# RWKV scan of a hybrid diffusion step: level products over all 128 rows, and a new issue order

## The reference

```python
def step(S, inp):
    r_t, w_t, k_t, v_t, kk_t, a_t = inp
    sa = jnp.einsum('bdhvk,bdhk->bdhv', S, -kk_t)
    S = (S * w_t[..., None, :] + sa[..., None] * (kk_t * a_t)[..., None, :]
         + v_t[..., None] * k_t[..., None, :])
    return S, jnp.einsum('bdhvk,bdhk->bdhv', S, r_t)
```

## Time and profile before

| | us |
|---|---|
| median of 3 runs (lowest, highest) | 4503.6 (4500.49, 4511.37) |
| the profiled execution | 4488.36 |
| its span, first to last instruction | 4486.5 |
| TensorE multiplying | 4088.9 (91%) |
| TensorE loading weights | 3518.4 (78%) |
| VectorE | 2644.1 (59%) |
| ScalarE | 1940.2 (43%) |
| GpSimd | 92.4 (2%) |
| mean granted TensorE clock | 0.966 of full speed |

### The profile page before, as it was taken

The page is one execution under the profiler, slowest core; times in us unless marked ns, Lnnn a source line. Parts: engine busy times, 40 slices in busy tenths (PEclk is TensorE's granted clock), DMA queues, the critical chain, the costliest instruction groups (busy, mean ns, idle before and its releaser), DMA issues. The chain is left out here.

```text
span 4486.5 us, 132472 instructions
## 1 busy us (share of the span) xinstructions
PE 4088.9 (91%) x58742; PEld 3518.4 (78%) x58742; DVE 2644.1 (59%) x4529; ACT 1940.2 (43%) x3640; POOL 92.4 (2%) x82
## 2 busy tenths in 40 slices
PE   6999978999988899899998999998999979999978
PEld 2888867888876799666668899886988868888858
DVE  6433557888866642455556433367524578888855
ACT  5333325666654531455554000045333256666642
POOL 0000000000110000000000000000000000001100
PEclk9999989999999899899999999999999989999989
DMA  8444765334434231100000222112345853334441
GB/s 314 145 127 134 221 206 147 101 104 103 99 68 158 79 70 41 53 1 1 2 15 24 98 95 71 43 62 69 114 124 174 255 163 107 103 107 100 92 151 59
DMA packets 541001, 470.96 MB, mean 105 GB/s; under 512 B 30096, under 2 KB 501264, under 8 KB 532752
## 3 DMA queue, kind: packets, MB, share of 16 engines
q1 hardware_dynamic: 389008, 386.96, 27.0%
q10 hardware_dynamic: 131840, 66.07, 5.1%
q0 software_dynamic: 19584, 9.44, 2.2%
HBM read 328.43 MB, written 128.71 MB: 102 GB/s over the span
## 5 line engine op out<-in xcount | busy, mean ns | idle before, releaser
L652 PE MATMUL ps<-big_r,stage_r 128*128 128x384 f32 x2976 | 638.8, 349 | 15.0 <-DVE big_r L914 13.6
L652 PEld LDWEIGHTS ps<-big_r,stage_r 128*128 128x128 f32 x2976 | 521.6, 189 | 69.2 <-issue 24.9
L2552 PE MATMUL ps<-big_r,w_out 128*128 128x384 f32 x2304 | 417.6, 341 | 36.1 <-DVE w_out L2668 35.8
L2552 PEld LDWEIGHTS ps<-big_r,w_out 128*128 128x128 f32 x2304 | 407.5, 191 | 44.6 <-DVE w_out L2668 38.8
L652 PE MATMUL ps<-big_r,w_slab_r 128*128 128x384 f32 x1488 | 340.6, 336 | 0.0
L369 PE MATMUL ps<-big_r,stage_r 128*128 128x384 f32 x1536 | 311.7, 337 | 13.2 <-DVE big_r L356 13.2
L2274 DVE TENSOR_REDUCE extra<-ps 128x1 f32<-128x1152 f32 (+1 forms) x144 | 177.7, 1234 | 204.0 <-PE ps L2179 204.0
L369 PEld LDWEIGHTS ps<-big_r,stage_r 128*128 128x128 f32 x1536 | 270.7, 189 | 27.8 <-issue 26.7
L1691 DVE COPY_PREDICATED arena<-arena,ps 128x128 f32<-128x128 uint32 x720 | 195.1, 328 | 123.6 <-PE ps L1305 121.1
L652 PEld LDWEIGHTS ps<-big_r,w_slab_r 128*128 128x128 f32 x1488 | 267.5, 189 | 0.0
L1513 ACT COPY arena<-ps 128x512 f32<-128x512 f32 x288 | 168.9, 586 | 205.1 <-PE ps L1319 204.9
(11 more groups left out here) (260 smaller groups left out, 8035.6 us busy)
## 6 DMA issues: line engine op xcount, KB each, us to landing
w_slab<-in_w SPq DMA_DIRECT2D x138, 512.0 KB, 3.3
arena<-scan_in SPq DMA_DIRECT2D x144, 320.0 KB, 3.7
arena<-scan_in SPq DMA_DIRECT2D x288, 128.0 KB, 3.7
scan_in<-x_resid ACTq DMA_DIRECT2D x48, 576.0 KB, 4.3
arena<-scan_in SPq DMA_DIRECT2D x48, 576.0 KB, 7.5
arena<-scan_in SPq DMA_DIRECT2D x144, 192.0 KB, 4.0
arena<-in_w_ada SPq DMA_DIRECT2D x24, 1024.0 KB, 5.9
x_resid<-in_w_ada SPq DMA_DIRECT2D x24, 1024.0 KB, 4.8
```

The costliest lines, as they stand in the source:

```text
L652: mm = pe.matmul(g.ps[:, 3 * s + c, 0:CW], w[:, k * P:(k + 1) * P], x[:, k, chunk(c)], start=k == i == 0, stop=k == NB - 1 and i == 2)
L2552: mm = pe.matmul(g.ps[:, bank(i, b), 0:wide[i]], w[:, b, k * P:(k + 1) * P], r, start=k == j == 0, stop=k == NB - 1 and j == 2)
```

## The change

The tile `xb` holds the inverse as a matrix with the two time halves on the diagonal and zeros beside them (cleared once by GpSimd), and `ba` holds the gram rows of both halves, one above the other, copied from `gr` by GpSimd (`copy_ba`, two copies of 64x512 for each pair). From level 2 on `level_u` is 8 products with 128 contracted rows, 64 output rows and 64 columns, and `level_x` (levels 2 to 4) likewise. `level_t` is 8 transposes of 64x128 in place of 4 of 128x128. `copy_x` becomes two copies, one for each half of the rows: 64x512 at level 1, 64x256 at levels 2 to 4. `level_w` at levels 2 to 4 is two masked copies of 64x256 instead of 128x128. Level 1's products, and `last_level_t`, stay. Both new tiles lie in the weight slab, which is idle in the scan.

```diff
+    xb = g.slab[:, 0, 0:1024]
+    ba = [g.slab[:, 1, 512 * i:512 * i + 512] for i in range(2)]
...
-            def level_u(q, k):
-                n = 1 << k
-                if k == 1:
-                    pe.wait_ge(x_ok, q + 1)
-                    if q:
-                        pe.wait_ge(w_ok, 10 * q)
-                if k == 5:
-                    pe.wait_ge(xa_ok, 4 * q + 4)
+            def first_u(q):
+                n = 2
+                pe.wait_ge(x_ok, q + 1)
+                if q:
+                    pe.wait_ge(w_ok, 10 * q)
+                    pe.wait_ge(xt_ok, 5 * q - 1)
...
                 for d, s in U8:
                     for h in range(2):
                         for p in range(2):
@@ -1307,28 +1308,50 @@
                                            strided(x, u * P + h * HD + d * n, (2 * n, 32 // n), (1, n), rows=HALVES[p]), start=True, stop=True)
                 mm.then_inc(u_mm, 1)
 
-            def level_x(q, k):
-                pe.wait_ge(w_ok, 10 * q + 2 * k)
-                if k == 1:
-                    pe.wait_ge(t1_ok, q + 1)
-                else:
-                    pe.wait_ge(xt_ok, 5 * q + k - 1)
+            def level_u(q, k):
+                n = 1 << k
+                if k == 2:
+                    pe.wait_ge(ba_ok, 2 * q + 2)
+                pe.wait_ge(xa_ok, 8 * q + 2 * k - 2)
+                for d, s in U8:
+                    for h in range(2):
+                        u = 2 * d + s
+                        mm = pe.matmul(strided(ps, u * HD, (1, HD), rows=HALVES[h]),
+                                       strided(ba[q % 2], (4 * h + u) * HD, (1, HD)),
+                                       strided(xb, u * P + h * HD + d * n, (512, 2), (2 * n, 32 // n), (1, n)), start=True, stop=True)
+                mm.then_inc(u_mm, 1)
+
+            def first_x(q):
+                pe.wait_ge(w_ok, 10 * q + 2)
+                pe.wait_ge(t1_ok, q + 1)
                 for d, s in U8:
                     for h in range(2):
                         for p in range(2):
                             mm = pe.matmul(strided(ps, h * 512 + (2 * d + s) * HD, (1, HD), rows=HALVES[p]),
                                            strided(xt[q % 2], lx(d, p, s), (1, HD), rows=HALVES[h]),
-                                           strided(wk(k), lx(d, p, s), (1, HD), rows=HALVES[h]), start=True, stop=True)
+                                           strided(wk(1), lx(d, p, s), (1, HD), rows=HALVES[h]), start=True, stop=True)
                 mm.then_inc(x_mm, 1)
 
+            def level_x(q, k):
+                pe.wait_ge(w_ok, 10 * q + 2 * k)
+                pe.wait_ge(xt_ok, 5 * q + k - 1)
+                for d, s in U8:
+                    for p in range(2):
+                        u = 2 * d + s
+                        mm = pe.matmul(strided(ps, 512 + u * HD, (1, HD), rows=HALVES[p]),
+                                       strided(xt[q % 2], lx(d, p, s), (1, HD)),
+                                       strided(wk(k), (2 * u + p) * HD, (1, HD)), start=True, stop=True)
+                mm.then_inc(x_mm, 1)
+
             def level_t(q, k):
 
-                if k < 4:
-                    pe.wait_ge(xa_ok, 4 * q + k)
                 if q and k == 1:
                     pe.wait_ge(xt_ok, 5 * q)
                 for d, s in U8:
-                    mm = pe.transpose(strided(ps, 2 * 512 + lx(d, 0, s), (P, 2), (1, HD)), strided(x, (2 * d + s) * P, (1, P)), g.ident[:, :])
+                    for p in range(2):
+                        u = 2 * d + s
+                        mm = pe.transpose(strided(ps, (1 + p) * 512 + u * HD, (1, HD)), strided(xb, p * 512 + u * P, (1, P), rows=HALVES[p]),
+                                          g.ident[HALVES[p], HALVES[p]])
                 mm.then_inc(t_mm, 1)
...
-            def tokens_v(q):
-                if q:
-                    pe.wait_ge(v_in[q % 4], 32 * loads(q, 4))
-                pe.wait_ge(t1_ok, q + 1)
-                for u in range(4):
-                    mm = pe.transpose(strided(ps, 3 * 512 + u * P, (1, P)), strided(vraw[q % 4], u * P, (1, P)), g.ident[:, :])
-                mm.then_inc(tok_mm, 1)
-
-            def tokens_bk(q):
-                if q >= 2:
+            def tokens(q, part):
+                if part == 0:
+                    if q:
+                        pe.wait_ge(v_in[q % 4], 32 * loads(q, 4))
+                    pe.wait_ge(t1_ok, q + 1)
+                if part == 2 and q >= 2:
                     pe.wait_ge(sum_ok, 2 * q - 2)
                 for u in range(4):
-                    mm = pe.transpose(strided(ps, 6 * 512 + u * P, (1, P)), strided(bk[q % 2], u * 256 + P, (1, P)), g.ident[:, :])
-                mm.then_inc(tok_mm, 1)
-                for u in range(4):
-                    mm = pe.transpose(strided(ps, 4 * 512 + u * P, (1, P)), strided(bk[q % 2], u * 256, (1, P)), g.ident[:, :])
+                    src = strided(vraw[q % 4], u * P, (1, P)) if part == 0 else strided(bk[q % 2], u * 256 + (part - 1) * P, (1, P))
+                    mm = pe.transpose(strided(ps, (3, 4, 6)[part] * 512 + u * P, (1, P)), src, g.ident[:, :])
                 mm.then_inc(tok_mm, 1)
...
             def copy_x(q, k):
+                n = 1 << k
                 act.wait_ge(x_mm, 4 * q + k)
-                A.copy(strided(x, 0, (HD, 2), (P, 4), (1, HD)), strided(ps, 0, (512, 2), (HD, 4), (1, HD))).then_inc(xa_ok, 1)
+                for p in range(2):
+                    rows = HALVES[p]
+                    if k == 1:
+                        if q == p == 0:
+                            act.wait_ge(blank_ok, 1)
+                        A.copy(strided(xb, p * 512, (HD, 2), (P, 4), (1, HD), rows=rows),
+                               strided(ps, 0, (512, 2), (HD, 4), (1, HD), rows=rows)).then_inc(xa_ok, 1)
+                    else:
+                        A.copy(strided(xb, p * 512, (256 + n, 2), (2 * n, P // n), (1, n), rows=rows),
+                               strided(ps, 512, (P, 2), (n, P // n), (1, n), rows=rows)).then_inc(xa_ok, 1)
 
...
-                    A.copy(strided(xt[q % 2], n, (256 - n, 2), (2 * n, P // n), (1, n)),
-                           strided(ps, 2 * 512 + n, (256 - n, 2), (2 * n, P // n), (1, n))).then_inc(xt_ok, 1)
+                    A.copy(strided(xt[q % 2], n, (P, 2), (256 - n, 2), (2 * n, HD // n), (1, n)),
+                           strided(ps, 512 + n, (512, 2), (P - n, 2), (2 * n, HD // n), (1, n))).then_inc(xt_ok, 1)
...
+            def chain_sa_half(c, step, d):
+                act.wait_ge(sa_mm, 2 * c + step + 1)
+                rows, t = HALVES[1 - tau(d, step)], tau(d, step)
+                A.copy(strided(sav[c % 2], t * 512 + d * 256, (HD, 2), (P, 2), (1, HD), rows=rows),
+                       strided(ps, 5 * 512 + d * P, (512, 2), (HD, 2), (1, HD), rows=rows)).then_inc(sav_ok, 1)
+
...
-                for p in range(2):
-                    V.copy_predicated(strided(wk(k), p * P, (256 + n, 2), (2 * n, HD // n), (1, n)),
-                                      bits(strided(level_mask, (k - 1) * P, (HD, 2), (n, HD // n), (1, n))),
-                                      strided(ps, p * 512, (HD, 2), (n, HD // n), (1, n))).then_inc(w_ok, 1)
+                for i in range(2):
+                    if k in (1, 5):
+                        src = strided(ps, i * 512, (HD, 2), (n, HD // n), (1, n)) if k == 1 else strided(ps, i * 32, (P, 2), (HD, 2), (1, 32))
+                        V.copy_predicated(strided(wk(k), i * P, (256 + n, 2), (2 * n, HD // n), (1, n)),
+                                          bits(strided(level_mask, (k - 1) * P, (HD, 2), (n, HD // n), (1, n))), src).then_inc(w_ok, 1)
+                    else:
+                        V.copy_predicated(strided(wk(k), i * 32, (256, 2), (HD, 4), (1, 32), rows=HALVES[i]),
+                                          bits(strided(level_mask, (k - 1) * P, (HD, 2), (0, 4), (1, 32), rows=HALVES[i])),
+                                          strided(ps, 0, (P, 2), (32, 4), (1, 32), rows=HALVES[i])).then_inc(w_ok, 1)
 
...
             nc.gpsimd.tensor_scalar(less, ch(g, "k_a", 8 * j, 8), -1.0, 1.0, ALU.mult, ALU.add).then_inc(less_ok, 1)
+
+            def copy_ba(q, t):
+                pool.wait_ge(g_ok, 4 * q + 2 * t + 2)
+                if q >= 2:
+                    pool.wait_ge(u_mm, 5 * q - 5)
+                rows = HALVES[1 - t]
+                nc.gpsimd.tensor_copy(strided(ba[q % 2], 0, (HD, 8), (1, HD), rows=rows),
+                                      strided(gr[q % 3], t * 1024, (P, 8), (1, HD), rows=rows)).then_inc(ba_ok, 1)
+
+            for q in range(2):
+                copy_ba(q, 0)
+                copy_ba(q, 1)
             for c in range(PAIRS):
+                if c + 2 < PAIRS:
+                    copy_ba(c + 2, 0)
+                    copy_ba(c + 2, 1)
                 if plain_stores(c) == 2:
                     continue
 
...
+            if k in (1, 5):
```

(24 more changed lines are left out.)

118 lines of the change are left out of this document (49 added, 69 removed).

## The result

The changed kernel takes 4390.6 us (median of 3 runs, 4390.2 to 4391.2), before 4503.6: a ratio of 0.9745 (95% interval 0.9726 to 0.9764), 2.5% less.

What follows compares the result with a forecast made beforehand. TensorE's list was taken to set the scan. Shortened to 16.4 us a pair, plus 1.0 new waits, 0.1 for VectorE and 0.95 hold-ups, it gave 18.45 for 18.82: -27 us over 72 pairs, 4476 us, range 4405 to 4550.

Steps and rivals of the forecast that it cites:

- my lower bound: TensorE's `level_t`: eight 64x128 transposes at 0.24 us if half the columns count half; 0.3 was taken, 0.47 the upper value.
- the sum: Three engine lists laid side by side: TensorE 16.4 us plus 1.0 of new waits, hold-ups added, 18.45 us a pair.
- The pair before: Scan period of the old kernel, 18.82 us: 17.3 without hold-ups in TensorE's groups, 1.5 lost to them.
- The clean pair, 17.5 forecast: Scan pair without hold-ups after the change: 17.5 us, 0.2 us longer than the old 17.3.
- 0.1 for a VectorE without slack: Added to the 17.4 us pair because VectorE would be busy for 16.8 of it: 0.1 us.
- 1.5 becomes 1.25 us: TensorE's hold-ups per pair shrink with its multiplies, 485 for 581: from 1.5 to 1.25 us.
- then 0.95: Hold-ups ahead of TensorE's new waits cost only what is over, taking a quarter off: 0.95 us a pair.
- (2): Hold-ups fall more than in proportion, or transposes take 0.24: 17.9 us a pair, 4437 us, down to 4410; chance 0.13.
- (4): VectorE's list takes over the scan: 19.1 to 19.4 us a pair, 4524 to 4546 us; chance 0.22.
- (5): GpSimd's copies disturb VectorE while they run: could be +0.7, so 19.2 us a pair, 4531 us; chance 0.08.
- (6): Undone row tiles on TensorE are missed, `u` groups double: +1.8 us a pair, +130 us, 4634 us; chance 0.03.
- takes 1.5 us out of a chain with slack: Putting `u` ahead of `t` in three levels cuts some 1.5 us from the level chain, grown from 12.5 to 14.9.

Runs made afterwards that it cites:

- e8: Kernel before, with two wide 256-column products into unused columns ahead of both the level 3 and level 4 products; 4581.9 us.
- e5: Kernel before, with two wide 256-column products into unused columns ahead of the level 4 product only; time grew by 43 us.
- e4: Changed kernel with each new level product split into two of 32 columns, same data and order; 4585.5 us.
- e7: Changed kernel with VectorE's 128x512 subtraction of the decays made by GpSimd; time the same as the changed kernel's, clean pair 16.83 us for 17.12.
- e6: Changed kernel with two wide 256-column products into unused columns ahead of the level 4 product; 4454.4 us.

## Why the prediction was wrong

- **Right: what bounds it, and the small terms.** TensorE's list set the pace. Multiplies a pair are 484 for 580, 96 fewer as counted. `level_w` takes 0.91 for 0.95, GpSimd's copy 0.61 for 0.7 and is hidden, TensorE waits for the two-part copies 11.1 us in 340 for some 15 in 380. The transposes take 0.24, my lower bound, where I took 0.3: 0.24 us a pair. TensorE's waits for data come to 1.0 us a pair (20.0 us in 340), as in the sum. The start of a scan costs nothing, as I had put it. The pair before was sized well, too: 17.3 and 1.5 us of hold-ups for 17.45 and 1.45.
- **The clean pair, 17.5 forecast, is 17.12.** The transposes are 0.24 of it; I had also added 0.1 for a VectorE without slack, which was not needed. The rest, 0.04, is open. That is 27 us.
- **The step that failed is "1.5 becomes 1.25 us", then 0.95.** I let the hold-ups fall with the count of instructions. Measured above the clean pair they are 0.34 us. The e8, e5 and e4 kernels show that the count is not what they follow: they fall when almost the same instructions are spread over a longer pair, and don't return with 596 multiplies at 60 records a us. Before, TensorE went through its list at 66 a us when nothing stopped it; the changed kernel asks for 57. Their 0.6 us below my value are 43 us. Together with the clean pair's 27 this makes the difference in the profiled executions, 4461 forecast for 4390.2.
- **The rival that came true is (2)**, with the lowest transposes and hold-ups that fall more than in proportion; I gave it 0.13 and priced it with 0.6 us of hold-ups at 4437, down to 4410; measured is 19 us less still, as both its clean pair (17.3) and its hold-ups were too large. Its "for" named the clock; a granted clock of 0.99 to 1.00 in both windows says that this is a small part.
- **(4) didn't come.** VectorE did get to 95%, but its waits for TensorE shrank with it, from 66 us to 21 between 900 and 1280 us; taking 0.6 us off it gained nothing in the time (e7). Neither list sets the pair alone: +1.06 us on TensorE's list costs 0.86 (e6), and -0.6 on VectorE's list gives 0.29 in the clean pair (e7).
- **(5) and (6) didn't come.** In the changed kernel hardly any of VectorE's products of two memory inputs runs beside GpSimd's copies, and the masked copies of a level that do take 0.437 us for 0.440 without. In e7 one such product runs beside GpSimd's subtraction and is no longer than before (0.683 us for 0.685), so the contention that the Trainium skill names (GPSIMD Engine Reference, Specifications) is not seen in it. Undoing the row tiles cost no time, since the groups over 64 rows had 16 products where the new ones have 8; at equal counts it does cost, as e4 shows, 57 ns a product for 29: there the rule of the Trainium skill (TensorEngine Tiling (Array Packing), When to Use Tiling) agrees with the runs.
- **The split between order and products** I had not forecast: the sum treated the order as something that takes 1.5 us out of a chain with slack. It is in fact what makes the products usable; without it they gain nothing, and over half of that is the wait for the level 4 copy that the new layout in PSUM brought.

**What stays open.** Where the hold-ups fall is a matter of the instruction stream. In the kernel before, from 932 us on, the number of weight loads between one and the next (two records each, so 127 loads are one block of the earlier trace rows) is

```text
380 380 379 633 380 127 379 253 380 127 633 633 252 254 127 506 380 506 253 380 253 253 127 126 633 253 254
```

all multiples of 126 to 127. So a hold-up stands at a block's border, but not at each one, and with the landing times above this shows that it is the next block that comes late. The Trainium skill (Runtime: NRT & Kernel Launch, Instruction fetch mechanics) gives 256 instructions a block, which fits, and calls the crossing mostly hidden; here the hold-ups cost 1.3 us in 18.9. Why a fetch starts later at some borders, and whether the mean pace or the bursts count (the old groups use 64 records in 0.46 us, the new ones 32), no run here separates.

## What to carry to other kernels

When an engine's list shows gaps inside a group, with no semaphore to wait for, take the distribution of the period and not its mean, and look at the distance between the gaps in instructions: if it is a multiple of one number, and the gaps end a fixed time after a packet of the instruction queue, the engine outruns its instructions, and the fix is work with fewer instructions for each microsecond. Such a loss isn't proportional to the count: here it fell from 1.30 to 0.38 us at a pace 14% lower. And test a change of products and a change of order each alone before crediting either, since here both were worth nothing without the other.

## What was not expected of the hardware

- To instructions that had not arrived TensorE lost 1.0 to 1.4 us a pair at 63 to 66 records a us (1.30 in 18.9 in the kernel before), and 0.2 to 0.6 us at 51 to 60. It went on 1.2 to 1.6 us after the block had landed.
- A product over 128 rows and 64 outputs costs 57 ns with 32 columns or 64; one over 64 rows and 64 outputs 29 ns.
- Eight 64x128 transposes into two banks take 0.24 us, four of 128x128 took 0.44 (0.59 less the 0.15 of a shape change).
- GpSimd copies 64x512 in 0.61 us but needs 1.76 us for a two-input subtraction of 128x512, and VectorE's instructions beside either are not longer than without.
